# Order of the high- and low-part products in the FFN gate and up projections of a two-layer decoder trunk

## What is computed

```
FFN_HIDDEN = -(-8 * D_MODEL // (3 * 256)) * 256        # 2816
...
  x = x + merged @ W_out
  x = x + SwiGLU(RMSNorm(x))       # silu(xn @ w_ffn_gate) * (xn @ w_ffn_up) @ w_ffn_down
```

## Time and profile before

| | |
|---|---|
| median of three timed runs | 854.2 us (854.05 to 854.21) |
| the profiled execution, its own time | 854.36 us |
| its span, first to last instruction | 852.5 us |
| mean granted TensorE clock | 1.000 |
| PE busy | 846.1 us (99% of the span) |
| DVE busy | 597.2 us (70%) |
| ACT busy | 500.1 us (59%) |
| POOL busy | 259.4 us (30%) |

### The profile page before, as it was taken

The page is one execution under the profiler, slowest core; times in us unless marked ns, Lnnn a source line. Parts: engine busy times, 40 slices in busy tenths (PEclk is TensorE's granted clock), DMA queues, the critical chain, the costliest instruction groups (busy, mean ns, idle before and its releaser), DMA issues.

```text
span 852.5 us, 12229 instructions
## 1 busy us (share of the span) xinstructions
PE 846.1 (99%) x4530; PEld 703.4 (83%) x4530; DVE 597.2 (70%) x932; ACT 500.1 (59%) x837; POOL 259.4 (30%) x253
## 2 busy tenths in 40 slices
PE   9999999999999999999999999999999999999998
PEld 5888887787888888888888788878788888888886
DVE  5566868657869888864555678676687698888552
ACT  6787654575457555553457775556654665556431
POOL 0086713004305444420000966310052144444100
PEclk9999999999999999999999999999999999999999
DMA  9755555444646655565565465455445465555652
GB/s 332 253 155 186 181 176 171 147 150 156 212 152 198 198 187 187 184 205 174 171 209 193 140 201 198 155 166 164 150 154 196 152 219 187 188 187 184 202 195 72
DMA packets 68442, 155.24 MB, mean 182 GB/s; under 512 B 5408, under 2 KB 7840, under 8 KB 68128
## 3 DMA queue, kind: packets, MB, share of 16 engines
q1 hardware_dynamic: 68096, 154.20, 55.4%
q10 hardware_dynamic: 288, 0.27, 0.1%
HBM read 153.40 MB, written 1.05 MB: 181 GB/s over the span
## 4 chain that ended last, share of the span: by engine, by line
PE 97%; DVE 1%; ACT 1%; DMA 1%; issue 0%; SPq 0%; ACTq 0%
PE acc L687 60%; PE acc L676 18%; PE acc L681 9%; PE att L767 2%; PE att L846 1%; PE att L821 1%; PE att L734 1%; PE att L759 1%; PE att L837 1%; DMA w_raw<-in_w_in 1%; PE att L805 0%; DVE xs L1253 0%; DVE w_lo L1184 0%; ACT sq_dump L1059 0%; PE att L859 0%
## 5 line engine op out<-in xcount | busy, mean ns | idle before, releaser
L1184 DVE TENSOR_TENSOR w_lo<-w_raw,w_hi 128x1024 fp32r<-128x1024 f32 (+1 forms) x276 | 357.0, 1304 | 124.0 <-ACT w_hi L954 122.8
L954 ACT ACTIVATE w_hi<-w_raw 128x1024 fp32r<-128x1024 f32 (+1 forms) x275 | 286.7, 1051 | 100.4 <-PE acc L687 73.4
L687 PE MATMUL acc<-w_hi,xt 128*128 128x512 f32 (+1 forms) x1024 | 261.1, 397 | 0.4 <-ACT w_hi L948 0.2
L687 PEld LDWEIGHTS acc<-w_hi,xt 128*128 128x128 f32 x1024 | 185.5, 188 | 39.1 <-issue 2.2
L676 PE MATMUL acc<-xt,w_hi 128*128 128x512 f32 x704 | 176.7, 393 | 0.5 <-DVE xt L1195 0.5
L1535 POOL TENSOR_TENSOR gate_up<-gate_up,rows 128x256 f32<-128x256 f32 x88 | 107.9, 1245 | 140.4 <-DVE gate_up L1258 122.6
L676 PEld LDWEIGHTS acc<-xt,w_hi 128*128 128x128 f32 x704 | 126.7, 189 | 23.6 <-issue 0.9
L687 PE MATMUL acc<-w_lo,xt 128*128 128x512 f32 (+1 forms) x512 | 136.0, 388 | 0.0
L687 PEld LDWEIGHTS acc<-w_lo,xt 128*128 128x128 f32 x512 | 96.0, 188 | 19.5
L681 PEld LDWEIGHTS acc<-xt,w_lo 128*128 128x128 f32 x704 | 96.1, 190 | 6.9
L681 PE MATMUL acc<-xt,w_lo 128*128 128x256 f32 x704 | 98.2, 282 | 0.0
(11 more groups left out here) (175 smaller groups left out, 807.7 us busy)
## 6 DMA issues: line engine op xcount, KB each, us to landing
w_raw<-in_w_ffn SPq DMA_DIRECT2D x88, 512.0 KB, 3.9
w_raw<-in_w_gate SPq DMA_DIRECT2D x64, 512.0 KB, 3.8
w_raw<-in_w_ffn_down SPq DMA_DIRECT2D x44, 512.0 KB, 3.8
w_raw<-in_w_in SPq DMA_DIRECT2D x39, 512.0 KB, 5.0
w_raw<-in_w_branch SPq DMA_DIRECT2D x16, 512.0 KB, 3.6
w_raw<-in_w_out SPq DMA_DIRECT2D x16, 512.0 KB, 3.5
bg<-in_b_gate SPq DMA_DIRECT2D x8, 512.0 KB, 5.6
w_raw<-in_w_in SPq DMA_DIRECT2D x8, 396.0 KB, 3.4
```

Source lines behind the costliest of these rows:

```text
L687: return pe.matmul(acc[bank0 + t][:, 0:N], x_part[:, k0 + k, t * P:(t + 1) * P], w_part[:, k, 0:N], start=first, stop=last)
L954: act.activation(w_hi[:, n % WR, :, 0:N], w_raw[:, n % RAW, :, 0:N], copy).then_inc(s_hi, 1)
L1184: dve.tensor_tensor(w_lo[:, n % WR, :, 0:N], w_raw[:, n % RAW, :, 0:N], w_hi[:, n % WR, :, 0:N].bitcast(F32), ALU.subtract).then_inc(s_lo, 1)
```

## The change

In `products`, for "ffn" chunks only, the wait for the low part of the chunk's weights moves ahead of the chunk's first product, and the two loops of eight products become one: each 512-column product of a slice of `w_hi` is followed at once by the 256-column product of the same slice of `w_lo` into the same PSUM bank. The number, the shapes and the operands of the products stay, and so do all other engines' programs.

```
                 if kind == "ffn":
                     wh4, wl4 = (w.rearrange("p a (b c) -> p (a b) c", b=2) for w in (wh, wl))
+                    pe.wait_ge(s_lo, n + 1)
                     for k in range(4):
                         if a == 0 and k % 2 == 0:
                             ready = ("pair", ("f", 2 * b + k // 2))
@@
                         for i in range(2):
                             pe.matmul(acc[bank0 + i][:, :], wh4[:, k, i * FC:(i + 1) * FC],
                                       xt[:, 4 * b + k, :, :].rearrange("p i t -> p (i t)"), start=first and k == 0, stop=False)
-                    pe.wait_ge(s_lo, n + 1)
-                    for k in range(4):
-                        for i in range(2):
                             mm = pe.matmul(acc[bank0 + i][:, 0:SEQ], wl4[:, k, i * FC:(i + 1) * FC], xt_hi[:, 4 * b + k, :],
                                            start=False, stop=last and k == 3)
                     mm.then_inc(s_ch, 1)
```

## The result

| | before | after |
|---|---|---|
| median | 854.2 us (854.05 to 854.47, 7 runs) | 856.59 us (854.53 to 857.4, 7 runs) |
| ratio after / before | | 1.0022, 95% interval 1.0012 to 1.0031 |
| profiled execution, its span | 854.36, 852.5 us | 857.09, 855.3 us |
| PE busy | 846.1 us | 849.0 us |

The kernel became 0.22% slower, where a gain of 2.2 us was forecast. The time lies in the range of 849.0 to 857.0 us, but on the other side of the kernel before: the direction is wrong. The single runs say more than the median: four lie between 856.59 and 857.4 us, three between 854.53 and 854.89, none between.

What follows compares the result with a forecast made beforehand. TensorE's product pace was taken as the bound: pairs at 0.346 us save 0.025 us per chunk, times 88 chunks -2.2 us, other terms nothing, so 854.2 - 2.2 = 852.0 us; 8 in 10 range 849.0 to 857.0.

Steps and rivals of the forecast that it cites:

- What bounds the kernel: Whole kernel: TensorE is busy 99% of the span; the ffn stage is bound by its product pace, 2.793 us per chunk.
- What a product costs: Ffn stage: 512 columns cost 0.2266 us, 256 cost 0.119, 0.006 above their columns; anything shorter than about 0.117 costs that.
- The rival of 0.340 us per pair: Ffn pairs: loads run further ahead and all are hidden, columns alone count, 847.8 us; chance 0.1.
- The order of the products: Ffn chunks: a pair takes 0.346 us, a chunk 2.768, 0.025 us less, times 88 chunks -2.2 us.
- a turn at half its price: Ffn chunks, within the slower rival: 0.0135 us per turn from short to long, +2.7 us, 857 us.
- The same bank twice: Ffn pairs: two consecutive products write one PSUM bank; claimed to cost nothing, +7 us if 0.01 us each.
- the earlier wait: Ffn chunk's first product: the wait for the weights' low part stands 1.84 us earlier; claimed to cost nothing.
- The cover of 2.35 us: Seventh ffn chunk, the tightest place: DVE's split ends 2.35 us before TensorE starts; a biting wait under 2 in 100.
- Slower: the turn from short to long: Ffn chunks: each turn costs 0.027 us, eight instead of one, +12 us, 866 us, or 857 at half; chance 0.15.
- 0.235 us or more for the long products: Ffn chunks: sign named for the slow rival, long products at this length behind every short one, instead of 0.2266 us.
- No gain: Ffn stage: the 0.027 us is spread over all products, a pair takes 0.349, 854.2 us; chance 0.25.
- Much faster: loads run further ahead: Ffn pairs: a long product's load is taken while the long one before the short still runs, 847.8 us; chance 0.1.

Runs made afterwards that it cites:

- e7: Kernel before, old order of eight long then eight short products, with short products set to 192, 224, 288, 320 and 384 columns by slice; 865.05 us.
- e8: Changed kernel's pairs with both widths set by slice: 512/512, 384/384, 256/256, 320/320 and 512/448 columns; 858.54 us.
- e2: Kernel before with only the wait for the weights' low part moved ahead of the chunk, products in the old order; 854.25 us, ratio 0.9998.
- e3: Changed kernel with, for each slice k, two long products and then two short ones instead of pairs; 853.89 us, ratio 0.9994.
- e4: Changed kernel with four long products and then four short ones, twice per chunk, instead of pairs; 855.23 us, ratio 1.0010.

## Why the prediction was wrong, point by point

**What bounds the kernel** was right: everything outside the ffn chunks stands still, and the pace of the products is all that counts.

**What a product costs** was misread, though the sum hardly rests on it. I read two things out of the earlier trace rows that e7 and e8 correct. I took half of a 512-column product, 0.113 us, for what 256 columns cost, and 0.117 for a floor set by the load, so that 0.119 looked like a load not quite hidden. In e8 a product in a stream of equals costs its columns at 2.4 GHz plus 0.0133 us at four widths, which is 0.120 for 256 columns, and the floor of a run of narrow ones is 0.112, below it. There was nothing for the long product to hide. `cumulate`, with its 128 columns, lies under that floor and says nothing about 256. The rival of 0.340 us per pair lies below the sum of the two, 0.3467, and no pair with 256 columns reached it. The sum of the forecast took 0.346 all the same, so this error did not turn the sign.

**The order of the products** is the step that failed, the term of -0.025 us per chunk, -2.2 us. I priced a pair as the sum of its parts at 0.346 us and let every pair have that price. The lower of the two paces is just that, 0.3467, and then the time is 852.5 to 853.2 us, 0.5 to 1.2 above the forecast of 852.0. The failed assumption is that there is one pace. Mixed widths can also settle at 0.3533, +0.054 us per chunk against the lower pace and +0.034 against the kernel before, and the 0.020 that the old order loses is less than the mean of 0 and 0.054. At a half each the sum would be 88 x (0.027 - 0.020) = +0.6 us; the seven runs of the result had four with both layers at the higher pace and three with one. That their median of 856.59 us lies in my range is luck: I had set its upper end at 857.0 for a turn at half its price, which is not what happened.

**The same bank twice** and **the earlier wait** were priced at nothing; e8 and e2 measured nothing. **The cover of 2.35 us** was never used up: no wait for the weights' low part stands among TensorE's waits.

**The rivals.** "Slower: the turn from short to long" had the right side and part of the mechanism, the 0.027 us behind a run as a sign that mixing widths costs, but the price does not go with the number of turns (e3, e4). The sign that I named for it, 0.235 us or more for the long products, did come: at the higher pace they take 0.241, 0.236 and 0.233 us in turn; it told of the pace and not of a price per turn. A pair's 0.0067 us lies under the 0.0096 from which I let it decide, because I credited the short product with 0.006 us that it did not have to give. "No gain" was right in size for the middle group of runs alone. "Much faster: loads run further ahead" did not come: at both paces each load in the steady part still starts 0.002 to 0.005 us behind the start of the product before its own. The sign against me stood in the rows: 1.84 us instead of 1.813 was a loss without a cause, and I let it vanish on the word of four turns of other widths.

**The chances.** 0.17 for slower was too little. With a loss in the rows that no wait or load explains, the honest price of a reordering runs both ways.

**Still open.** What makes a mixed stream settle at one of two paces is not shown. The runs show that no wait stands in it, that the granted clock is 1.00 at both, that the two paces are the same in all traces, and that the products before decide which one holds. That other engines' traffic has no part in it is argued from this, not tested. Nor is it shown what decides it at the stage's start. In every profile of the pairs the chunk (0, 0) has the higher pace, and the courses part in the chunk (0, 1), the one chunk of the stage that starts behind a real wait, for DVE's `xt`; it takes 2.85 us where it runs at the lower pace and 2.89 where it runs at the higher, and "rows" then turns the one into the other. That the moment of the wait's release decides is argued. Whether a stage without "rows" at that place would keep its first pace no run tried.

## What to carry to other kernels

Before reordering products to hide weight loads, measure the floor of a run of narrow products and the cost of a column in a run of equal ones: here a product costs columns / 2.4 GHz + 0.013 us and a run of narrow ones stops at 0.112 us, so from 256 columns on there is nothing to hide. Keep widths equal in long stretches where that is free; a mixed order should be judged by several profiles, on more than one occasion, and by the groups in its times, for one median can be a draw between two paces. A loss in the rows that has no wait to explain it belongs in the range with both signs.

## What the hardware showed that was not expected

A stream of 512- and 256-column products in turn settles at 0.3467 or at 0.3533 us per pair and stays there for more than 300 pairs. One added product of 384 columns moved it from the second to the first (and left it at the first where it met that), one of 128 columns moved it from the first to the second, and those of 256, met at the second, and 512, met at the first, left it alone. Four products of 128 columns in a row, the step "rows", turned either pace into the other in all 18 layers. At the higher pace the pattern repeats over three pairs, 1.06 us, while a chunk has eight. Long streams of equal products, of any of four widths and with the same banks and buffers in turn, had one pace only in e8's profile. The fixed 0.0133 us per product holds for this kernel's fp32r products. The Trainium skill ("TensorE: Matmul & The Clock Gate", section "Back-to-back issue gap") states N / 2.4 + 2.5 ns, 216 ns for 512 columns. No fp32r stream here comes down to that, but the last two of the kernel's 12 warm-up products, bf16 with 512 columns, start 0.216 us apart in the profile of the kernel before.
